# Split weights stored 128 bytes apart, and 512-column products taken in runs of 64 bytes

## The reference, cut to what matters

```python
for l in range(DEPTH):                                   # first block, two layers
    n = rms_norm(h, mix_norm_g[l])
    proj = jnp.einsum("btd,de->bte", n, w_in[l])         # q, k, v, indexer, rnn, conv, gates
    ...                                                  # attention over selected keys, rg-lru, conformer conv
    h = h + jnp.einsum("btd,de->bte", merged, w_out[l])
    f = rms_norm(h, ffn_norm_g[l])
    a = silu(einsum("btd,df->btf", f, w_ffn_gate[l])) * einsum("btd,df->btf", f, w_ffn_up[l])
    h = h + jnp.einsum("btf,fd->btd", a, w_ffn_down[l])
# second block: swiglu, neighbourhood attention and S5 scan, swiglu, gated p @ ple_w_proj, rms_norm
```

## Time and profile before

| | |
|---|---|
| median of 3 runs | 3559.79 us (3556.57 to 3565.98) |
| the profiled execution | 3565.33 us, its span 3563.4 us |
| mean granted TensorE clock | 0.987 |
| busy in the span | PE 96%, PEld 84%, DVE 67%, POOL 57%, ACT 28% |
| TensorE instructions | 19988 matmuls, as many weight loads |

### The profile page before, as it was taken

The page is one execution under the profiler, slowest core; times in us unless marked ns, Lnnn a source line. Parts: engine busy times, 40 slices in busy tenths (PEclk is TensorE's granted clock), DMA queues, the critical chain, the costliest instruction groups (busy, mean ns, idle before and its releaser), DMA issues.

```text
span 3563.4 us, 49689 instructions
## 1 busy us (share of the span) xinstructions
PE 3435.1 (96%) x19988; PEld 2982.4 (84%) x19988; DVE 2382.9 (67%) x3005; ACT 993.5 (28%) x1716; POOL 2042.8 (57%) x1100
## 2 busy tenths in 40 slices
PE   7999899999999999999999999999999999999997
PEld 7899789999999879977778778878887875788886
DVE  6787898877833578888888863386336765743435
ACT  4406442312110241654232110111114444322201
POOL 4355334655766645533566766677665662466674
PEclk9999999999999999999999999999999999999998
DMA  3122111222323322211223432343335441223332
GB/s 137 60 89 78 48 48 66 83 89 96 126 89 100 111 68 89 81 55 56 83 86 106 147 127 101 100 147 127 100 104 203 142 154 52 91 94 100 101 106 71
DMA packets 96898, 348.29 MB, mean 98 GB/s; under 512 B 10848, under 2 KB 13152, under 8 KB 93664
## 3 DMA queue, kind: packets, MB, share of 16 engines
q1 hardware_dynamic: 80064, 289.44, 24.7%
q10 hardware_dynamic: 16672, 56.70, 4.2%
HBM read 322.32 MB, written 23.79 MB: 97 GB/s over the span
## 4 chain that ended last, share of the span: by engine, by line
PE 75%; DVE 18%; ACT 3%; issue 2%; DMA 1%; POOL 0%; ACTq 0%; DVEq 0%; POOLq 0%
PE acc L521 23%; PE acc L522 22%; PE acc L524 22%; DVE cu L2088 3%; PE acc L783 1%; PE aux L835 1%; DVE ptmp L2291 1%; PE acc L864 1%; PE aux L710 1%; DVE pap L2291 1%; DVE fpr L1821 1%; DVE mtmp L1875 1%; DVE pcp L2291 1%; PE aux L690 1%; PE aux L754 1%
## 5 line engine op out<-in xcount | busy, mean ns | idle before, releaser
L494 POOL TENSOR_SCALAR whi<-raw 128x1024 fp32r<-128x1024 f32 x548 | 624.9, 1140 | 1447.0 <-PE acc L524 1425.9
L496 POOL TENSOR_TENSOR wlo<-raw,whi 128x1024 fp32r<-128x1024 f32 x548 | 1418.0, 2588 | 45.7
L521 PE MATMUL acc<-nhi_s,whi 128*128 128x512 f32 x1568 | 619.8, 395 | 19.6 <-DVE fpr L1818 6.1
L524 PE MATMUL acc<-nhi_s,wlo 128*128 128x512 f32 x1568 | 612.0, 390 | 0.0
L522 PE MATMUL acc<-nlo_s,whi 128*128 128x512 f32 x1568 | 612.0, 390 | 0.0
L521 PE MATMUL acc<-bhi,whi 128*128 128x264 f32 (+1 forms) x1864 | 555.9, 314 | 12.3 <-ACT tqg L1149 5.5
L522 PE MATMUL acc<-blo,whi 128*128 128x264 f32 (+1 forms) x1864 | 542.0, 307 | 0.0
L524 PE MATMUL acc<-bhi,wlo 128*128 128x264 f32 (+1 forms) x1864 | 447.0, 306 | 0.0
L521 PEld LDWEIGHTS acc<-bhi,whi 128*128 128x128 f32 x1864 | 354.1, 190 | 43.4 <-issue 10.5
L521 PEld LDWEIGHTS acc<-nhi_s,whi 128*128 128x128 f32 x1568 | 295.3, 188 | 92.7 <-issue 13.5
L522 PEld LDWEIGHTS acc<-blo,whi 128*128 128x128 f32 x1864 | 353.8, 190 | 14.9
(11 more groups left out here) (410 smaller groups left out, 5865.1 us busy)
## 6 DMA issues: line engine op xcount, KB each, us to landing
raw<-in_w SPq DMA_DIRECT2D x548, 512.0 KB, 3.3
kept_cp<-pcp ACTq DMA_DIRECT2D x4, 1280.0 KB, 6.4
cp<-kept_cp ACTq DMA_DIRECT2D x4, 1280.0 KB, 10.2
kept_ap<-pap ACTq DMA_DIRECT2D x4, 1024.0 KB, 6.1
kept_cs<-pcs ACTq DMA_DIRECT2D x4, 1024.0 KB, 6.4
ap__151<-kept_ap ACTq DMA_DIRECT2D x4, 1024.0 KB, 6.9
cs__162<-kept_cs ACTq DMA_DIRECT2D x4, 1024.0 KB, 6.8
merge_gates<-gout ACTq DMA_DIRECT2D x16, 256.0 KB, 2.2
```

The lines of the kernel that those rows point to most:

```text
L494: pool.tensor_scalar(hi, w, 1.0, 0.0, ALU.mult, ALU.add).then_inc(sem("w_hi"), 1)
L496: pool.tensor_tensor(lo, w, hi.bitcast(F32), ALU.subtract).then_inc(sem("w_split"), 1)
L521: pe.matmul(acc[s][:, f, 0:TH], hi, xh[:, f * TH:(f + 1) * TH], start=a, stop=False)
L524: m = pe.matmul(acc[s][:, f, 0:TH], lo, xh[:, f * TH:(f + 1) * TH], start=False, stop=z)
```

## The change

`whi` and `wlo` become one array `wparts` of [column of the panel, high or low, slot, panel]. In each partition a column of the panel has 128 bytes: the first 64 hold its high part for two slots of eight panels, the second 64 its low part. The 128 weights of one panel are therefore read with a step of 128 bytes, and the high parts of all panels lie in the even runs of 64 bytes, the low parts in the odd ones. GpSimd's writes of both parts, and its read of the high part, go through that layout too.

Operands with rows of 512 elements (`R.even`) are streamed in another order: the 32 runs of 16 elements (64 bytes) are taken as all odd runs and then all even ones, or the reverse, and the columns of the PSUM sum are addressed in the same order (`runs`, `three`). A matmul behind which a high part is loaded takes the odd runs first, and one behind which a low part is loaded takes the even runs first. The tiles of 264 columns and the slices of 528-element rows are streamed as before, with weights in the new layout. `h` is placed at a multiple of 256 bytes, so every large array is aligned to 64 bytes, and `zeros` shrinks to the 16 columns that are used.

```diff
+RUN = 16
...
+        zeros = fixed("zeros", [P, META])
+        place[0] = (place[0] + 255) // 256 * 256
...
-        whi = fixed("whi", [P, 2, BLK * P], F32R)
-        wlo = fixed("wlo", [P, 2, BLK * P], F32R)
-        zeros = fixed("zeros", [P, 128])
+        wparts = fixed("wparts", [P, P, 2, 2, BLK], F32R)
...
-                hi = whi[:, s].rearrange("p (a c) -> p a c", a=BLK)
-                lo = wlo[:, s].rearrange("p (a c) -> p a c", a=BLK)
+                hi, lo = (wparts[:, :, z, s, :].rearrange("p c a -> p a c") for z in range(2))
                 pool.tensor_scalar(hi, w, 1.0, 0.0, ALU.mult, ALU.add).then_inc(sem("w_hi"), 1)
                 pool.wait_ge(sem("w_hi"), b + 1)
                 pool.tensor_tensor(lo, w, hi.bitcast(F32), ALU.subtract).then_inc(sem("w_split"), 1)
...
+            def weights(slot, j):
+                return wparts[:, :, 0, slot, j], wparts[:, :, 1, slot, j]
+
+            def runs(x, odd_first):
+                v = x.rearrange("p (c z e) -> p z c e", z=2, e=RUN)
+                return v[:, ::-1] if odd_first else v
+
+            def three(out, hi, lo, xh, xl, a, z):
+                pe.matmul(runs(out, True), hi, runs(xh, True), start=a, stop=False)
+                pe.matmul(runs(out, False), hi, runs(xl, False), start=False, stop=False)
+                return pe.matmul(runs(out, True), lo, runs(xh, True), start=False, stop=z)
...
-                    hi = whi[:, slot, (w0 + j) * P:(w0 + j + 1) * P]
-                    lo = wlo[:, slot, (w0 + j) * P:(w0 + j + 1) * P]
+                    hi, lo = weights(slot, w0 + j)
                     xh, xl = rhs(j0 + j)
                     a, z = first and j == 0, last and j == nk - 1
+                    if rhs.even:
+                        out = acc[s][:, 0, :]
+                        m = three(out, hi, lo, xh, xl, a, z)
+                        continue
...
-            def R(hi, lo, T, o=0):
-                return lambda j: (hi[:, j, o:o + T], lo[:, j, o:o + T])
+            class R:
+                def __init__(self, hi, lo, T, o=0):
+                    self.hi, self.lo, self.T, self.o = hi, lo, T, o
+                    self.even = hi.shape[-1] == SEQ
```

More of the change, by code:

```diff
@@ L562, in short, with __call__ @@
                 for j in range(nk):
[L563 to L568, removed]
-                return m
-            def R(hi, lo, T, o=0):
-                return lambda j: (hi[:, j, o:o + T], lo[:, j, o:o + T])
+                    m = three(bank(n), *weights(slot, w0 + j), *rhs(j), j == 0, j == nk - 1)
+                return m
+            class R:
+                def __init__(self, hi, lo, T, o=0):
+                    self.hi, self.lo, self.T, self.o = hi, lo, T, o
+                    self.even = hi.shape[-1] == SEQ
+                def __call__(self, j):
+                    return self.hi[:, j, self.o:self.o + self.T], self.lo[:, j, self.o:self.o + self.T]
             def sumsq(i):
```

## The result

| | before | after |
|---|---|---|
| median | 3562.89 us (4 runs, 3556.57 to 3567.8) | 4795.12 us (4 runs, 4791.13 to 4798.31) |
| ratio | | 1.3459, 95% interval 1.3433 to 1.3486 |
| span of the profiled execution | 3563.4 us | 4796.4 us |
| mean granted TensorE clock | 0.987 | 0.981 |

The forecast of 3517 us was wrong, and the range too. What came is the fourth rival, which I had put at 4500 us with a chance of 0.12.

What follows compares the result with a forecast made beforehand. TensorE was taken as the bound, busy 96% of the span, so the distance between matmul starts counts. Terms -73 + 0 + 30 = -43 us, with 0 for alignment, gave a 3517 us median; range 3465 to 3850.

Steps and rivals of the forecast that it cites:

- fourth rival: Weight loads: with a step they take 221 ns and pace 264-column matmuls, 943 us more, 4500 us; chance 0.12.
- part 2: 264-column and unsorted 512-column products: order kept, weights read 128 bytes apart, taken as 0.
- Part 1: 512-column products with rows of 512: loads and streams stop meeting, up to 81 us saved, 73 taken.
- the same 4.6 ns: Extra start distance of 512-column matmuls whose operand begins 64 bytes later in 2112-byte rows: 231.5 against 226.9 ns.
- Part 3: GpSimd's split with stepped accesses: +1.0 us a block, mostly hidden in its wait for TensorE, 30 us lost.
- first rival: GpSimd becomes the bound: a split 2.0 us longer gives 3713 us, 2.8 about 3950; chance 0.23.
- Part 4: Alignment and zeros: arrays move by a few hundred bytes, no instruction added, 0.
- third rival: Stepped weight reads collide more with unsorted streams: 26 ns on 10656 matmuls, 277 us, 3794 us; chance 0.09.

Runs made afterwards that it cites:

- experiment 6: Kernel before with high and low weights of two panels interleaved, a panel's columns 16 bytes apart, streams in plain order: 4859.19 us.
- experiment 1: Changed kernel with GpSimd writing contiguous panels, TensorE alone reading weights with a 64-byte step, streams in plain order: 4544.57 us.
- experiment 5: Kernel before with high and low weights alternating element by element, a panel's columns 8 bytes apart, plain order: 3618.12 us.
- experiment 3: Changed kernel with the 512 columns streamed in plain order: 4783.82 us.
- experiment 4: Changed kernel with contiguous weights as before, keeping the order in runs and the places of the arrays: 3641.06 us, ratio 1.022.
- Experiment 2: Changed kernel with only GpSimd's side stepped (64 bytes), TensorE reading neighbouring elements, plain order: 3936.14 us, ratio 1.1047.
- experiment 11: Kernel before with only the change's places: zeros cut to 16 columns, h on a multiple of 256: 3563.04 us, ratio 1.0005.

## Why the prediction was wrong

**What failed first is the value in part 2.** The prediction wrote of the stepped weight load: "I take 0". It had a price at the end of the same paragraph (+0.84 ns a column, a load of 221 ns) and even the sum, 4500 us, as the fourth rival, and then left that rival out of the range. Measured is +0.82 ns a column and a distance of 225.0 ns: 982 us where the rival had 943. That the price met within 3% is luck. The 0.84 is what ScalarE takes for an element without a step; what the step adds in the same rows is (430 - 304)/128 = 0.98 ns. With that the rival would have had a load of 240 ns and some 4690 us. ScalarE's step there is 16 bytes, and at 16 bytes TensorE's load did pay (307 - 186)/128 = 0.95 ns a column (experiment 6); so ScalarE's rows did say what was coming. The 0 had no row behind it: its only ground was that half of the columns lie where the weights are, as before, which speaks of collisions and not of what a step costs the load itself. The Trainium skill (Advanced Engine Details and Errata, Memory Cachelines) stood beside the fourth rival and excepts no engine from its rule. Experiments 1, 5 and 6 agree with it. Most of the 295 us between 4500 and 4795 are terms that the rival put at nothing: the slower sorted matmuls, TensorE's waits and the clock.

**The rival said that the sorted ones gain nothing; they lost.** They went from 226.9 to 245.2 ns, 127 us. 9 ns of that are the load with a step in plain order (experiment 1), most of the rest is the order, worth 7 to 8 ns on top of a stepped load (experiment 3) and 13 ns alone (experiment 4).

**Part 1 counted a gain that no run found.** I took nine tenths of 11.6 ns off each 512-column matmul because loads and streams would meet no more in the same 64 bytes. The interference is real, but its period is 256 bytes, the kernel before stands at the best of the offsets for both operands that were moved, and no offset or order that was tried brought these matmuls below 226.6 ns. Keeping the two apart while the load is fast wasn't tried. The distance that I compared with, eight plain float32 matmuls, says what an unhurried stream leaves over, not that addresses make the difference. Rivals for the same 4.6 ns should have been asked for: it showed that an address can cost something, and I read it as if another could pay.

**Part 3, the split: term and cover.** +1.0 us a block was taken, +1.45 us came (1140 to 2134 ns and 2588 to 3040 ns): within what the text allowed. At +1.45 the first rival, in which GpSimd becomes the bound, asks for 302 x (1.45 - 1.25) = 60 us. Experiment 2 measured 373 us. The assumption that a longer split hides as long as it fits into GpSimd's wait for TensorE is what failed. GpSimd's busy time also blocks VectorE, and TensorE waits for VectorE: 182 of the 251 us of idle time that experiment 2 added. The clock came on top, 0.960 instead of 0.987. Behind slow loads the same split cost 239 us instead of 373, and the order 11 instead of 78. That is why the parts measured alone, 982 + 373 + 78 = 1433 us, are more than the 1232 us of the whole.

**Part 4 was right:** the places cost nothing (experiment 11).

**The third rival** blamed the right part of the change by the wrong mechanism: collisions with the stream, at 0.4 ns for half of the columns (26 ns a load). Measured is a longer load, 0.82 ns for every column at its minimum. Whatever collisions come on top are small beside it: at most 9.4 ns a plain 512-column matmul in experiment 1.

**What stays open.** 11 ns of each 512-column matmul, over 213.3 of streaming and 2 of its own, are there at the best offset too, and no run made them less. Which of GpSimd's stepped accesses makes up how much of the 452 ns of the TENSOR_TENSOR wasn't separated. Nor is it known why the matmuls of the 8-byte kernel lose 6.4 ns, or where between 8 and 16 bytes the load's price begins. Weights in a layout with contiguous pairs or quadruples of columns and a long step between them weren't tried.

## What to carry to other kernels

Before an operand gets a step, count how many of its elements lie in each 16 bytes, for every engine that touches it: one in 16 bytes cost TensorE's loads and GpSimd's writes 0.8 to 1 ns an element here, two cost 0.05 to 0.07, and a load that outlasts its matmul sets TensorE's pace. Cover for a longer GpSimd instruction has to be looked for twice, in GpSimd's own waits and in the VectorE instructions that run beside it. Where TensorE's busy share can't tell two kernels apart, as here (96% both), the distance of its starts can.

## What the runs showed of the hardware that I had not expected

- A weight load of 128 float32 columns: 186 ns contiguous, 192 with a step of 8 bytes, 307 with 16, 291 with 64 or 128.
- GpSimd's TENSOR_SCALAR over 1024 elements nearly doubles when its write has a step of 16 bytes or more (1140 to 2134 ns, 2187 at 16), with 8 bytes it takes 1212.
- A stepped split alone makes the kernel 373 us slower, with 251 us more of TensorE's idle time, 182 of them in waits for VectorE. VectorE's long instructions end 0.3 to 0.6 us after GpSimd's, in the kernel before as well.
- The place of weights against the moving operand is worth 6 to 6.5 ns a 512-column matmul: 226.6 to 227.0 ns at 0 and 256 bytes, 232.6 to 233.5 at 64 and 128.
- Streaming every other 64 bytes costs 13 ns a 512-column matmul, every other 256 bytes nothing.
